# Semaphore waits in place of four engine barriers, and stick and sparse values as 400 columns

## The reference

```python
p = rmsnorm(x, norm_mix) @ w_in
y = concat([retention_mixer(p[..., :2048]), rwkv7_mixer(p[..., 2048:])])
x = x + y @ w_out
x = x + memory_cross_attention(rmsnorm(x, norm_xattn), rmsnorm(mem, norm_mem), xattn_w_q, xattn_w_kv, xattn_w_o)
x = rmsnorm(x + square(relu(rmsnorm(x, norm_mlp) @ mlp_w_up)) @ mlp_w_down, norm_final)
```

```python
h = rmsnorm_2(x, norm_mix_g) * (1.0 + sc_a) + sh_a
(a_q, a_k, a_v, b_q, b_k, b_v, b_f, c_q, c_k, c_v,
 d_q, d_kc, d_vc, d_ks, d_vs, d_kw, d_vw, d_g) = split(h @ w_in_2)
o_c = stick_breaking_attention(c_q, c_k, c_v)     # log_sigmoid, running sum of the tail, exp, times c_v
x = x + gt_a * (concat([o_a, o_b, o_c, o_d]) @ w_out_2)
```

## Time and profile before

| | us |
|---|---|
| median of 3 runs | 1644.75 |
| lowest and highest | 1641.38, 1645.51 |
| the profiled execution | 1644.14 |
| its span (first to last instruction) | 1642.3 |
| PE busy in the span | 1589.6 (97%) |
| DVE busy | 888.2 (54%) |
| ACT busy | 669.4 (41%) |

### The profile page before, as it was taken

One profiled execution on the slowest core, in us unless ns is written; L12 is line 12 of the kernel. 1 busy time (PEld: TensorE's weight loads), 2 busy tenths in 40 slices (PEclk: granted clock), 3 DMA queues, 4 the chain that ended last, 5 costly groups with the idle time before them and its releaser, 6 DMA issues.

```text
span 1642.3 us, 27109 instructions
## 1 busy us (share of the span) xinstructions
PE 1589.6 (97%) x11727; PEld 1285.9 (78%) x11727; DVE 888.2 (54%) x1386; ACT 669.4 (41%) x1005; POOL 120.6 (7%) x138
## 2 busy tenths in 40 slices
PE   7999999998999999999999999999899999999998
PEld 5856778776895798888888898777568888888887
DVE  5455586442634364555454654436875766555644
ACT  4316843324334264334141254656883532221210
POOL 1310106000000010000000020012300000000000
PEclk9999999999999999999999999999999999999999
DMA  7611223320630335536453533321003243333322
GB/s 241 185 52 52 76 89 100 113 85 30 198 132 23 128 123 187 183 105 228 128 179 128 179 87 109 77 77 52 2 27 103 62 118 85 96 103 103 94 78 86
DMA packets 154073, 176.66 MB, mean 108 GB/s; under 512 B 14600, under 2 KB 111506, under 8 KB 153570
## 3 DMA queue, kind: packets, MB, share of 16 engines
q1 hardware_dynamic: 145004, 162.24, 31.0%
q10 hardware_dynamic: 8950, 12.69, 2.6%
HBM read 168.31 MB, written 8.43 MB: 108 GB/s over the span
## 4 chain that ended last, share of the span: by engine, by line
PE 85%; DVE 7%; ACT 5%; issue 2%; DMA 1%; ACTq 0%; SPq 0%; DVEq 0%; POOL 0%
PE ps L397 63%; PE ps L848 4%; PE ps L1471 4%; PE ps L824 1%; PE ps L2066 1%; PE ps L3135 1%; DMA sb_arena<-sb_arena 1%; DVE weights_low L420 1%; PE ps L2892 1%; ACT weights_high L417 1%; PE ps L2880 1%; PE ps L2912 1%; PE ps L1049 1%; PE ps L765 1%; DVE sb_hT L2988 1%
## 5 line engine op out<-in xcount | busy, mean ns | idle before, releaser
L420 DVE TENSOR_TENSOR weights_low<-sb_weights_raw,weights_high 128x2048 fp32r<-128x2048 f32 (+2 forms) x117 | 263.9, 2255 | 260.2 <-ACT weights_high L417 260.0
L397 PE MATMUL ps<-left_high,weights_high 128*128 128x512 f32 (+1 forms) x888 | 352.0, 396 | 2.3 <-DVE left_low L718 2.1
L397 PE MATMUL ps<-left_low,weights_high 128*128 128x512 f32 (+1 forms) x888 | 345.9, 390 | 0.0
L397 PE MATMUL ps<-left_high,weights_low 128*128 128x512 f32 (+1 forms) x888 | 345.9, 390 | 0.0
L417 ACT CAST weights_high<-sb_weights_raw 128x2048 fp32r<-128x2048 f32 (+2 forms) x117 | 219.4, 1875 | 299.3 <-PE ps L397 261.6
L397 PEld LDWEIGHTS ps<-left_high,weights_high 128*128 128x128 f32 (+1 forms) x888 | 166.0, 187 | 47.5 <-issue 9.2
L397 PEld LDWEIGHTS ps<-left_high,weights_low 128*128 128x128 f32 (+1 forms) x888 | 166.0, 187 | 36.0
L397 PEld LDWEIGHTS ps<-left_low,weights_high 128*128 128x128 f32 (+1 forms) x888 | 166.1, 187 | 35.5 <-issue 1.7
L397 PE MATMUL ps<-weights_high,hidden_high 128*128 128x512 f32 x432 | 169.1, 391 | 0.0
L397 PE MATMUL ps<-weights_high,hidden_low 128*128 128x512 f32 x432 | 168.2, 389 | 0.0
L397 PE MATMUL ps<-weights_low,hidden_high 128*128 128x512 f32 x432 | 168.1, 389 | 0.0
(11 more groups left out here) (445 smaller groups left out, 2463.1 us busy)
## 6 DMA issues: line engine op xcount, KB each, us to landing
sb_weights_raw<-in_w_in SPq DMA_DIRECT2D x25, 1024.0 KB, 5.2
sb_yT<-in_ada_w SPq DMA_DIRECT2D x24, 1024.0 KB, 5.3
sb_weights_raw<-in_ffn_w_up SPq DMA_DIRECT2D x44, 512.0 KB, 4.8
sb_weights_raw<-in_mlp_w_up SPq DMA_DIRECT2D x16, 1024.0 KB, 5.8
sb_weights_raw<-in_mlp_w_down SPq DMA_DIRECT2D x16, 1024.0 KB, 7.5
sb_weights_raw<-in_ffn_w_down SPq DMA_DIRECT2D x10, 1024.0 KB, 5.1
sb_weights_raw<-in_xattn_w_kv SPq DMA_DIRECT2D x8, 1024.0 KB, 5.3
sb_weights_raw<-in_w_out SPq DMA_DIRECT2D x6, 1024.0 KB, 5.1
```

What stands on the lines that cost most here:

```text
L397: last = nc.tensor.matmul(o, lhsT, rhs, start=b["first"] and i == 0, stop=b["last"] and i == len(pairs) - 1)
L420: nc.vector.tensor_tensor(l[:, 0:n], raw[:, 0:n], h[:, 0:n].bitcast(F32), ALU.subtract).then_inc(w_low, 1)
```

## The change

It has two parts.

First, `stage_end` and its semaphore are gone at all four places. Where an engine needs something of another there, it now waits for that alone: the first six grams each for the bank that they write (`INV_BANK_READ`), DVE's grams for the masks of the inverse, PE's scan for the copies of all grams, ACT's output norms for the scan's output, `w_out`'s first chunk for four subtractions of `RET_LOW`, and PE's cross attention for the eight banks of `w_q`. The first unit of `kv` in the gram loop moves to its end.

Second, the 256 and the 144 columns become one row block of 400 for each of the four token tiles. Its weights, 8 k-tiles of 400, don't fit one slot, so they are two chunks of 4 k-tiles: `upper` (U) and `lower` (L). Each is used for tiles 0 and 1, then, as a chunk marked `again` that loads nothing and keeps its slot, for tiles 2 and 3. A tile's bank stays open from U to L. The order becomes U and L on tiles 0, 1, then U and L on tiles 2, 3, then KV, then f89, and so on; the `fill` counts in `front_*` and `stick_*` change with it.

```diff
-    def stage_end(self):
-
-        self.eng.drain().then_inc(self.stage_sem, 1)
-        self.wait_ge(self.stage_sem, self.count(self.stage_sem, 3))
...
-                if mod:
+                if ch.get("again"):
+                    ch["parts_slot"], ch["parts"] = ch["again"]["parts_slot"], ch["again"]["parts"]
+                    parts_free[ch["parts_slot"]] = acc
+                elif mod:
...
         def grams_pe(pe, dense):
             for n, (u, lhsT, rhs, dst, mask) in enumerate(ALL_GRAMS):
-                if n >= N_GRAM_BANKS:
+                if n < N_GRAM_BANKS:
+                    pe.wait_ge(*INV_BANK_READ[n])
+                else:
...
-                if n % 3 == 2:
+                if n % 3 == 2 and n > 2:
                     fill(dense, 1)
...
+            pe.wait_ge(gram_by_dve, 4 * NPAIR)
+            pe.wait_ge(gram_by_act, 2 * NPAIR)
             for u in range(NPAIR):
                 last = rhs_of_values(0, u)
...
+        def stick_and_sparse_rows():
+
+            columns = (2052, 2308), (2756, 2820), (2884, 2960), (1536, 1540)
+
+            def blocks(half, tiles):
+                return [by_token(0, ROWS_W, h_rows(t), "dve", dve_copy_to(VB[:, t, ROWS_AT:ROWS_AT + ROWS_W]), nk=4,
+                                 k0=4 * half, first=half == 0, last=half == 1) for t in tiles]
+
+            upper, lower = (chunk_of([W2K[:, 4 * half:4 * half + 4, x:y] for x, y in columns], blocks(half, (0, 1)))
+                            for half in range(2))
+            return [upper, lower] + [dict(pieces=[], again=ch, nk=4, width=ROWS_W, blocks=blocks(half, (2, 3)))
+                                     for half, ch in enumerate((upper, lower))]
...
-            chunk_of(w2((2052, 2308)), trow(0, 256, 512)),
-
+            *stick_and_sparse_rows(),
...
-            chunk_of(w2((2756, 2820), (2884, 2960), (1536, 1540)), trow(0, 144, 768)),
...
             scores(0)
-            fill(dense, 4)
+            fill(dense, 6)
             tails(0, 0)
...
             scores(1)
-            fill(dense, 4)
+            fill(dense, 5)
             tails(1, 0)
             fill(dense, 1)
             tails(1, 1)
-            fill(dense, 2)
+            fill(dense, 1)
             times_v(1)
...
+            split_weights(v, "dve", w_in_2[8]["index"])
             exponents(1, 0)
-            split_weights(v, "dve", w_in_2[6]["index"])
...
-            pe.stage_end()
+            for bank in range(8):
+                pe.wait_ge(*banks_after(w_q)[0][bank])
             pe.wait_ge(mem_moved, 16 + 16 * 4 + 48)
```

More of the change, by code:

```diff
@@ L139, with __init__ @@
 class Side:
-    def __init__(self, eng, stage_sem):
-        self.eng, self.wait_ge, self.stage_sem = eng, eng.wait_ge, stage_sem
+    def __init__(self, eng):
+        self.eng, self.wait_ge = eng, eng.wait_ge
         self.seen = {}
@@ L408, in split_weights @@
                 side.split += 1
-                if ch.get("kind"):
+                if ch.get("kind") or ch.get("again"):
                     continue
@@ L1724, in grams_dve @@
         def grams_dve(v, dense):
+            v.wait_ge(inv_masked, 5 * NPAIR)
             for n, (u, lhsT, rhs, dst, mask) in enumerate(ALL_GRAMS):
@@ L2001, in build_program @@
         w_out = in_halves(A["w_out"][0], ((0, 1, 2, 3), (4, 5, 6, 7)), mixed_rows, add_half)
-        w_out[0]["left"] = 0
+        w_out[0]["left"] = 4
         (sa_scores, sa_shifted, sa_exp, sa_probs, sa_turned, sa_kept, sa_pv, sa_out_kept) = (sem("attn_" + n) for n in (
@@ L2520, in w2 @@
             return [W2K[:, :, x:y] for x, y in ranges]
+        ROWS_AT, ROWS_W = 512, 400
+        def stick_and_sparse_rows():
[7 more added lines that the diff above has]
+                                     for half, ch in enumerate((upper, lower))]
         w_in_2 = [
@@ L2614, in sparse_act @@
             store_gates_act(a)
-            columns_kept(a, 5)
+            columns_kept(a, 7)
             a.wait_ge(keys_spread, 32)
@@ L2647, in sparse_dve @@
             v.wait_ge(dve_order, pe_kept)
-            columns_kept(v, 3)
+            columns_kept(v, 6)
             for i in range(2):
@@ L2696, in norms_act @@
         def norms_act(a, dense):
-            for i, (tiles, SQ, n, kept) in enumerate(((QK[:, 4:8, :], SQ_FOX, 64, 7), (QK[:, 0:4, :], SQ_DIFF, 32, 9))):
+            for i, (tiles, SQ, n, kept) in enumerate(((QK[:, 4:8, :], SQ_FOX, 64, 9), (QK[:, 0:4, :], SQ_DIFF, 32, 11))):
                 columns_kept(a, kept)
@@ L2727, in front_pe @@
             dense = product_steps(pe, w_in_2[2:], 2)
-            fill(dense, 4)
+            fill(dense, 2)
             pe.wait_ge(bank_free["act"], w_in_2[1]["blocks"][-1]["free"])
@@ L2736, in front_act @@
             dense = evac_steps(a, "act", w_in_2)
-            fill(dense, 12)
+            fill(dense, 10)
             for i in range(2):
@@ L3205, in stick_act @@
             fill(dense, 4)
-            split_weights(a, "act", w_in_2[6]["index"])
+            split_weights(a, "act", w_in_2[8]["index"])
             weights(1, 0)
@@ L3247, in stick_dve @@
             scaled(0, 1)
-            fill(dense, 2)
+            fill(dense, 4)
             softplus(0, 0)
@@ L3627, in _ @@
             skew_bias_sp(sp)
-            stream_weights(sp, STREAM[w_q[2]["index"]:w_in_2[4]["index"]])
+            stream_weights(sp, STREAM[w_q[2]["index"]:w_in_2[7]["index"]])
             load_bias_sp(sp, range(4))
-            stream_weights(sp, STREAM[w_in_2[4]["index"]:w_in_2[7]["index"]])
+            stream_weights(sp, STREAM[w_in_2[7]["index"]:w_in_2[9]["index"]])
             load_bias_sp(sp, range(4, 8))
-            stream_weights(sp, STREAM[w_in_2[7]["index"]:])
+            stream_weights(sp, STREAM[w_in_2[9]["index"]:])
             for n in range(2 * NT):
@@ L3640, in _ @@
         def _(eng):
-            a = Side(eng, stage_sem)
+            a = Side(eng)
             a.split = 0
@@ L3666, in _ @@
         def _(eng):
-            v = Side(eng, stage_sem)
+            v = Side(eng)
             v.split = 0
@@ L3690, in _ @@
         def _(eng):
-            g = Side(eng, stage_sem)
+            g = Side(eng)
             rstd_pool(g, NORM_1, by_dve=(0, 2))
@@ L3704, in _ @@
         def _(eng):
-            pe = Side(eng, stage_sem)
+            pe = Side(eng)
             start_pe(pe)
```

18 lines of the change are left out of this document (4 added, 14 removed).

## The result

| | us |
|---|---|
| changed kernel, median of 22 runs | 1646.09 |
| kernel before, median of 22 runs beside them | 1641.49 |
| ratio, 95% interval | 1.0032 (1.0023 to 1.0041) |
| predicted | 1648.7 (1640.0 to 1653.0) |
| profiled execution, span after (before) | 1645.1 (1642.3) |

The account below looks back on a forecast made before the run. PE, busy for 97% of the span, was taken to bound the kernel. 1644.14 - 2.3 (barriers) - 3.6 (columns) + 8.8 (late f67) + 1.7 (clock) = 1648.7 us, range 1640.0 to 1653.0.

Parts of the forecast that it names:

- The late f67: After scores(1): PE waits 6.0 us for f67's weights_low, then 1.05 ahead of times_v(1); L2578 comes 8.8 us later.
- The columns: Stick part, first half: 400-column products save 4.8 us, a new bank wait costs 1.4, a 0.2 wait goes; -3.6.
- in proportion: Rival on the 400 columns: a matmul's price goes with its columns alone, saving nothing; 1653.5 us, chance 0.02.
- The barriers: Four barriers removed: -2.3 us, of 3.2 us PE idle time there; bounds -3.2 and 0.
- first three places: First three barriers, the third ahead of w_out's first product: -0.3, -1.0 and -1.0 us.
- fourth place: Barrier ahead of the cross attention: PE waited 0.7 us, but needs the bank of ACT's copy L2191; gain 0.
- signs of being wrong: f67's subtraction ending before s + 14 (s: scores(1) start), 400-column pitch above 0.2, or barriers' idle time under other names.
- The clock: Behind PE's 6 us wait for f67 the clock falls to half, losing 1.7 us; bounds 0 and 3.4.
- 3.4 us stretch of the earlier trace: Half-clock stretch (granted clock 0.50) after PE's 2.1 us idle time ahead of L824, basis for the 1.7 us loss.
- rival of a longer fall: Behind f67's wait the clock loses 3.4 us, not 1.7, and falls again later for another 1.7; 1652.1 us, chance 0.18.
- the same: Whole kernel: time within about 0.3%, or 4.9 us, of no change; chance 0.46.
- slower: Whole kernel: slower by over 0.3%, a time over 1649.7 us; chance 0.44.

Follow-up runs that it names:

- experiments with f67's unit and two_keys: Two runs on the changed kernel: f67's first unit behind tails(1, 0) again, ratio 0.9968; two_keys' copies and DMA issues ahead of both magnitudes of g = 1, 1.0022.
- the barriers alone: Kernel before with only the first part of the change, waits for the data instead of barriers: 1637.53 us, ratio 0.9980.
- f67 moved alone: Changed kernel with f67's first unit put back behind tails(1, 0), nothing else: 1635.85 us, ratio 0.9968.
- all three fixes: Changed kernel with f67's first unit behind tails(1, 0), two_keys ahead of the magnitudes, first tile's copy between the two scaled: 1634.29 us, ratio 0.9961.

## Why the prediction was right

**The late f67 (+8.8), right.** It was the term that decided the sign. The step of +11.16 less 2.6 of clock is 8.6. The subtraction starts 17.31 us after scores(1) (17.29 predicted), PE's wait is 6.2 us (6.0), the one ahead of times_v(1) 1.1 (1.05). Here are ACT, with two_keys between the halves, and f67's cast:

```profile
1022.47 0.58 ACT L2517 COPY sb_arena<-ps 64x512 f32<-64x512 f32 x1
...
1024.36 1.24 ACT L3188 ACTIVATE sb_yT<-ps 128x1280 f32<-128x1280 f32 x1 [1.31 <-issue]
...
1032.15 1.90 ACT L414 CAST weights_high<-sb_weights_raw 128x2048 fp32r<-128x2048 f32 x1
```

And DVE with f67's subtraction:

```profile
1034.36 2.28 DVE L417 TENSOR_TENSOR weights_low<-sb_weights_raw,weights_high 128x2048 fp32r<-128x2048 f32 x1
```

It could be forecast this closely because each duration on the path from scores(1) to the subtraction stood in the trace of before, and the order list said what had been put in between. The experiments with f67's unit and two_keys show both halves of the cause.

**The columns (-4.8 + 1.4 - 0.2), right.** The pitch is 4.38 / 24 = 0.1825 (0.1806), the wait for the bank 1.3 (1.4), the stretch up to scores(1) -3.52 (-3.6). The rival "in proportion" is out: 96 x 0.1825 = 17.5 us against the 22.16 of before. The Trainium skill's rule on the start-to-start time (page "TensorE: Matmul & The Clock Gate", the section named in the prediction) gave an estimate of 0.169 us here and almost no saving; the measurement is 8% over it at 400 columns, and what it misses most here is the products of 144 columns, at 0.1108. One reading in the working is wrong: from the wait for the bank to tails(0, 0) PE has not 13 us of products left but 8.98 (the 48 at 985.89); 13 is all 72. The conclusion held, as no wait came at L3153.

**The barriers (-2.3), right in sign, the size open.** By w_out the changed kernel is 1.9 us ahead (2.25 from its own start), near the 2.3 of the first three places. This is partly luck, as the clock in the scan differs between the two profiles; like traces give 0.6 to 2.4. At the fourth place I took 0, and it gives some back: L2048 waits 0.9 us for ACT's copy, where the barrier cost 0.7. There the idle time came back under another name, one of the signs of being wrong. The run times of the barriers alone lie around -3.3.

**The clock (+1.7), too small.** I took the 3.4 us stretch of the earlier trace rows; behind the wait of 6.2 us the window from 1035 to 1042 shows 0.52, and f67's unit took 5.35 us in place of 2.77, so 2.6. It lay inside the bounds of 0 to 3.4. The rival of a longer fall is half true: the stretch was as long as that around 530, but its first part fell in the wait, tails(1, 0) behind it took no longer than elsewhere (4.33), and there was no second fall at L2596 (3.70 in both kernels). Why the clock stayed low for longer than behind L824 is not shown.

**The level.** The absolute 1648.7 was 2.6 us over the median because the kernel before, in 22 runs, has its median at 1641.49 and not at 1644.75; that the stated range of 13 us held the result is owed in part to its width. The move itself was +4.0 predicted and +5.2 (3.8 to 6.7) measured by the ratio; the terms as measured, with -1.8 for the barriers, add up to -1.8 - 3.5 + 8.6 + 2.6 = +5.9. The chances had "the same" a little ahead of "slower"; measured it is just over the bound of 0.3%, with an interval on both sides of it.

## What to carry to other kernels

When work is moved in one engine's list, follow the operand that the moved instruction needs on the two engines that make it, and compare the times from a common event: here PE needed f67's low parts 13.6 us after the scores, and ACT and DVE could not have them before 19.6. Saving 4.8 us of matmul pitch was easy to see, and the price of one unit standing one place too early was twice that. After such a change look for short work that fits in front of the wait: putting the tails back there turned +0.32% into -0.32%.

## What the runs showed of the hardware

The granted clock fell at places in one execution and not in another, with the same instructions and the same idle time ahead of them. PE is idle for 2.1 us ahead of L821 (L824 before) in both kernels; before, the clock was at the 1.2 GHz level after it, in the changed kernel it was at full speed (1.00 from 946 to 951). Where PE's products follow each other such a fall is a loss: the eight products at 530 took 6.77 us in one execution and 5.40 in the other, 1.4 us, as much as a barrier.

Behind PE's wait for f67 it was low in all the profiles that had the wait, with 6.2 us (units of 5.35, 5.49 and 4.38 us) or with 3.8 us (4.61), and at full speed where the wait was filled or gone (3.01 and 2.99).

In the scan it is the other way round, and that was not expected: the six traces with a fall there have the shorter stretch, by 0.3 to 3.3 us between kernels without barriers. What they have less of is idle time of PE for which the profile shows no wait ("issue"). These are its lines in the scan with f67 moved alone (no fall), then with all three fixes (a fall); up to the cross attention the two kernels are the same:

```profile
PE ps L1815 <- issue: 2.9, 3, 1.8
...
PE ps L1810 <- issue: 1.2, 1, 1.2
```

```profile
PE ps L1815 <- issue: 1.2, 1, 1.2
```

Over all ten traces it is 3.2 to 4.1 us without a fall and 1.0 to 2.0 with one. Which of the two brings the other, and why, no run here shows.

So a term under 2 us is not read from one span less another, but from one shared event to the next; and where the stretch itself differs between executions, as the scan does, one pair of traces is not enough.
